# The RWKV rounds of a hybrid decoder layer: a new order of operations on TensorE, VectorE and ScalarE

## What is computed

```python
def step(s, inp):                      # s: state of a head, 64 x 64
    r_t, w_t, k_t, v_t, a_t, b_t = inp
    sa = jnp.einsum('bhij,bhj->bhi', s, a_t)
    s = s * w_t[:, :, None, :] + sa[..., None] * b_t[:, :, None, :] + v_t[..., None] * k_t[:, :, None, :]
    return s, jnp.einsum('bhij,bhj->bhi', s, r_t)
...
y = ((y - mean) * lax.rsqrt(var + R_LN_EPS)).reshape(bsz, t, R_WIDTH) * ln_w + ln_b
bonus = jnp.sum(rh * kh * r_k, axis=-1, keepdims=True) * vh
y = y + bonus.reshape(bsz, t, R_WIDTH)
return (y * g) @ w_out, p[:, -1], s_fin
```

## Time and profile before

| | |
|---|---|
| median of 3 runs | 4114.88 us (4113.28 to 4115.73) |
| the profiled execution | 4111.77 us |
| its span | 4109.3 us |
| TensorE / VectorE / ScalarE busy, share of the span | 93% / 58% / 38% |
| rounds of the RWKV stage | from 2139 us to 2721 us of the span |

### The profile page before, as it was taken

How to read it: one execution, slowest core, us unless ns; L and a number is a source line. 1 busy time by engine, 2 the same in 40 slices (tenths; PEclk the granted TensorE clock), 3 DMA queues, 4 the chain that set the end, 5 groups by cost and what they waited for, 6 DMA issues and landing times. The chain is left out here.

```text
span 4109.3 us, 87073 instructions
## 1 busy us (share of the span) xinstructions
PE 3808.0 (93%) x37206; PEld 3472.0 (84%) x37206; DVE 2370.5 (58%) x4637; ACT 1574.3 (38%) x2857; POOL 195.6 (5%) x203
## 2 busy tenths in 40 slices
PE   8999999999999999889978888879999999999998
PEld 4889999998888889889966666669876899999997
DVE  4445646432588885358966666646643564444446
ACT  3113232232476653334426666544522431111112
POOL 0000000000011111010000000000111100000000
PEclk9999999999999999999989999989999999999999
DMA  5323222243565543655641111042323131111112
GB/s 209 91 87 94 89 89 89 83 112 120 157 155 165 155 136 117 184 150 192 224 145 32 33 36 36 24 162 96 115 89 121 48 103 47 42 44 50 42 32 85
DMA packets 375550, 418.84 MB, mean 102 GB/s; under 512 B 50474, under 2 KB 317276, under 8 KB 374300
## 3 DMA queue, kind: packets, MB, share of 16 engines
q1 hardware_dynamic: 362927, 368.14, 29.3%
q0 software_dynamic: 7632, 27.84, 2.3%
q10 hardware_dynamic: 4608, 17.30, 1.1%
HBM read 289.10 MB, written 121.77 MB: 100 GB/s over the span
## 5 line engine op out<-in xcount | busy, mean ns | idle before, releaser
L248 PE MATMUL bank<-xn_hi,pw_whi 128*128 128x352 f32 (+1 forms) x2184 | 728.8, 334 | 14.9 <-ACT ring L261 7.2
L248 PE MATMUL bank<-xn_hi,pw_wlo 128*128 128x352 f32 (+1 forms) x2184 | 705.8, 323 | 0.0
L248 PE MATMUL bank<-xn_lo,pw_whi 128*128 128x352 f32 (+1 forms) x2184 | 705.0, 323 | 0.0
L248 PEld LDWEIGHTS bank<-xn_hi,pw_whi 128*128 128x128 f32 (+1 forms) x2184 | 411.7, 189 | 38.8 <-issue 24.2
L248 PEld LDWEIGHTS bank<-xn_lo,pw_whi 128*128 128x128 f32 (+1 forms) x2184 | 413.0, 189 | 3.1 <-issue 1.9
L248 PEld LDWEIGHTS bank<-xn_hi,pw_wlo 128*128 128x128 f32 (+1 forms) x2184 | 411.8, 189 | 1.3
L261 ACT ACTIVATE ring<-bank 128x352 f32<-128x352 f32 (+1 forms) x273 | 126.0, 462 | 433.9 <-PE bank L248 433.2
L3214 PE MATMUL bank<-bx_hi,bp_whi 128*128 128x384 f32 (+1 forms) x768 | 269.6, 351 | 18.4 <-DVE bx_lo L3275 15.6
L1804 PE MATMUL bank<-sum_x_hi,pw_whi 128*128 128x352 f32 x768 | 254.1, 331 | 31.1 <-DVE sum_x_lo L1795 13.9
L233 DVE TENSOR_TENSOR pw_wlo<-ring,pw_whi 128x1024 fp32r<-128x1024 f32 (+1 forms) x92 | 117.9, 1282 | 240.1 <-ACT pw_whi L226 239.7
L3851 PE MATMUL bank<-bx_hi,bp_whi 128*128 128x384 f32 (+1 forms) x768 | 251.2, 327 | 4.7 <-issue 4.7
(11 more groups left out here) (719 smaller groups left out, 10690.8 us busy)
## 6 DMA issues: line engine op xcount, KB each, us to landing
ring<-in_w_in_dram SPq DMA_DIRECT2D x90, 512.0 KB, 4.8
proj_scratch<-ring SPq DMA_DIRECT2D x66, 528.0 KB, 3.0
mm_all<-proj_scratch SPq DMA_DIRECT2D x40, 512.0 KB, 6.0
mm_all<-acum_scratch SPq DMA_DIRECT2D x32, 512.0 KB, 6.7
ring<-in_mlp_w_dram SPq DMA_DIRECT2D x16, 1024.0 KB, 5.4
ring<-in_mlp_w_dram SPq DMA_DIRECT2D x32, 512.0 KB, 3.5
gates_scratch<-ring SPq DMA_DIRECT2D x24, 528.0 KB, 6.4
merged_scratch<-sum_gate ACTq DMA_DIRECT2D x24, 528.0 KB, 4.9
```

The lines of the kernel that those rows point to most:

```text
L248: last = self.nc.tensor.matmul(ps[0:n, 0:m], w[:, q, 0:n], self.pair[x][:, q, t0:t0 + m], start=q == 0 and j == 0, stop=q == KD - 1 and j ...
```

## The change

Every part's operations are placed by tables of ticks, 280 to a round, instead of 28 slots, and each engine has a table of its own. A tick below zero (or above 279) puts the operation into the iteration before (or behind). Operations that stood together under one slot are parted: the three masks of the gram step on VectorE (`part` 0 to 2), the two copies of `rows_kb` and of `rows_vd` on ScalarE, the two exponentials of the decay (`ex`, `decays`), the logarithm and the exponential behind it (`k_log`, `k_rs`, with a semaphore in the place of a drain), the square and the copy of `Finish`. The first gram of a round, the first copies and sigmoids of `Prepare` and its first product are issued at the end of the iteration before. The receptance and the key change their order on VectorE and their temporaries. The instructions, their shapes and their number stay; the SyncE and GpSimd programs stay. In the diff one line of three of the tables stands for them; the conversions of the other methods are of the same kind as the two shown.

```diff
-SLOTS = 28
+TICKS = 280
...
-INVERSION = [("gram", "v", 0), ("rows_kb", "a", 3), ("rows_vd", "va", 5), ("square", "va", 7), ("fourth", "va", 10), ("eighth", "v", 13),
-             ("by8", "v", 15), ("turn", "va", 17), ("cross1", "v", 20), ("cross2", "v", 22)]
...
+def at(**ops):
+
+    return {tick % TICKS: (name, -(tick // TICKS)) for name, tick in ops.items()}
...
+SCAN_DVE = at_chunks({(0, 0): 6, (1, 0): 35, (2, 0): 66, (3, 0): 95, (4, 0): 125, (5, 0): 155, (6, 0): 185, (7, 0): 215})
...
+PREPARE_PE = at(lw=-24, la=7, k_sum=75, bon=137)
+PREPARE_ACT = at(key_scale=-54, decay=-31, receptance_scale=-27, value_scale=-24, a=-20, k_sq=17, a_scaled=42, ex=63, decays=104, k_log=118, k_rs=127)
...
-    def scalar(self, act, r, slot):
-        if not 0 <= r < ROUNDS:
+    def scalar(self, act, r, tick):
+        op, ahead = PREPARE_ACT.get(tick, (None, 0))
+        r += ahead
+        if not 0 <= r < ROUNDS or op is None:
             return
...
-        elif slot == 7:
+        elif op == "ex":
             self.nc.scalar.preload_act_table_set("natural_log_exp_and_others")
             act.wait_ge(self.cum, r + 1)
             activation(v.ex[:, :, 1:1 + RC], T[1].rearrange("p (c t) -> p c t", t=RC), ACT.Exp, scale=-KAPPA)
+        elif op == "decays":
             activation(T[4], T[1], ACT.Exp, scale=KAPPA).then_inc(self.decays, 1)
-        elif slot == 8:
+        elif op == "k_log":
             act.wait_ge(self.k_sum, r + 1)
-            activation(T[5], bank[:, :], ACT.Ln, bias=k.eps[:, 1:2])
-            act.drain()
+            activation(T[5], bank[:, :], ACT.Ln, bias=k.eps[:, 1:2]).then_inc(self.k_logged, 1)
+        else:
+            act.wait_ge(self.k_logged, r + 1)
             activation(T[5], T[5], ACT.Exp, scale=-0.5).then_inc(self.k_rs, 1)
...
         @block.scalar
         def _(act):
-            for q in range(-1, ROUNDS + 2):
-                for slot in range(SLOTS):
-                    invert.scalar(act, q, slot)
-                    scan.scalar(act, q - 1, slot, finish.stored)
-                    prepare.scalar(act, q + 1, slot)
-                    finish.scalar(act, q - 2, slot)
+            for q in range(-2, ROUNDS + 3):
+                for tick in range(TICKS):
+                    invert.scalar(act, q, tick)
+                    scan.scalar(act, q - 1, tick, finish.stored)
+                    prepare.scalar(act, q + 1, tick)
+                    finish.scalar(act, q - 2, tick)
```

More of the change, by code:

```diff
@@ L1121, with at_chunks @@
-EACH = {w: sum(w in who for _, who, _ in INVERSION) for w in "va"}
+INVERSION = [("gram", "v"), ("rows_kb", "a"), ("rows_vd", "va"), ("square", "va"), ("fourth", "va"), ("eighth", "v"), ("by8", "v"),
+             ("turn", "va"), ("cross1", "v"), ("cross2", "v")]
+STEP = {name: s for s, (name, _) in enumerate(INVERSION)}
+EACH = {w: sum(w in who for _, who in INVERSION) for w in "va"}
+def at(**ops):
+    return {tick % TICKS: (name, -(tick // TICKS)) for name, tick in ops.items()}
+def at_chunks(ops):
+    return {tick % TICKS: (step, -(tick // TICKS)) for step, tick in ops.items()}
@@ new lines, in at_both @@
+def at_both(*ops):
+    return {tick % TICKS: ((name, p, part), -(tick // TICKS)) for name, part, ticks in ops for p, tick in enumerate(ticks)}
+INVERT_PE = at_both(("gram", 0, (-21, 6)), ("rows_kb", 0, (11, 29)), ("rows_vd", 0, (34, 61)), ("square", 0, (90, 96)), ("fourth", 0, (118, 130)),
+                    ("eighth", 0, (148, 154)), ("by8", 0, (162, 170)), ("turn", 0, (180, 191)), ("cross1", 0, (204, 220)),
+                    ("cross2", 0, (225, 253)))
+INVERT_DVE = at_both(("gram", 0, (-8, 12)), ("gram", 1, (5, 16)), ("gram", 2, (10, 20)), ("rows_vd", 0, (73, 89)), ("square", 0, (114, 123)),
+                     ("fourth", 0, (133, 145)), ("eighth", 0, (153, 156)), ("eighth", 1, (154, 157)), ("by8", 0, (165, 182)),
+                     ("turn", 0, (199, 204)), ("cross1", 0, (206, 220)), ("cross1", 1, (216, 234)), ("cross2", 0, (236, 260)))
@@ L1124, in evacuated @@
+PREPARE_DVE = at(zero=-84, key=-12, receptance=27, value=31, cum=65, k_a=72, bon=124, k_n=128, b_a=143, bonus=147, AR_r=167, PC=168, AR_a=183, B=186,
+                 K=200)
+FINISH_PE = at(mean=155, var=195, gate=226)
+FINISH_ACT = at(square=169, centre=186, log=219, rstd=220)
+FINISH_DVE = at(scale=229, bias=233, gate=235)
 def evacuated(r, s, who):
-    return r * EACH[who] + sum(who in w for _, w, _ in INVERSION[:s + 1])
+    return r * EACH[who] + sum(who in w for _, w in INVERSION[:s + 1])
@@ L1171, in tensor @@
         at, T = slice(n * RW, (n + 1) * RW), v.T
-        if slot == 0:
+        if op == "lw":
             if r >= 1:
@@ L1392, in vector @@
-        last.then_inc(self.vs[p], 1)
-    def scalar(self, act, r, slot):
-        if not 0 <= r < ROUNDS or slot not in STEPS:
+        if part == 0:
+            if "a" in INVERSION[s][1]:
+                dve.wait_ge(self.as_[p], evacuated(r, s, "a"))
+            else:
+                dve.wait_ge(self.pes[p], r * len(INVERSION) + s + 1)
+        if step == "gram" and part == 0:
+            tt(v.ABR[:, w, c, :], wide(b0), mask(v.m_a), ALU.mult)
+        elif step == "gram" and part == 1:
+            tt(x.O[:, :, :], wide(b0)[:, :, 0:RC], mask(v.m_cross), ALU.mult)
+        elif step == "gram":
+            tt(v.KX[:, w, c, :], wide(b1), mask(v.m_k), ALU.mult).then_inc(self.vs[p], 1)
+        elif step == "rows_vd":
+            plus_one(x.X, 0).then_inc(self.vs[p], 1)
+        elif step in ("square", "fourth"):
+            plus_one(x.P, 1).then_inc(self.vs[p], 1)
+        elif step in ("eighth", "cross1") and part == 0:
+            plus_one(x.P, 0)
+        elif step in ("eighth", "cross1"):
+            copy(halves(x.X), self.product(p, 1)).then_inc(self.vs[p], 1)
+        elif step == "by8":
+            copy(halves(x.X), self.product(p, 0)).then_inc(self.vs[p], 1)
+        elif step == "turn":
+            plus_one(x.P, 0).then_inc(self.vs[p], 1)
+        else:
+            copy(v.N[:, w, c, :].rearrange("p (q e) n -> p e q n", e=2),
+                 self.product(p, 0).rearrange("p e (q n) -> p e q n", n=RC)).then_inc(self.vs[p], 1)
@@ L1396, in scalar @@
+    def scalar(self, act, r, tick):
+        if tick not in INVERT_ACT:
             return
-        s, p = STEPS[slot]
-        if "a" not in INVERSION[s][1]:
+        op, ahead = INVERT_ACT[tick]
+        r += ahead
+        if not 0 <= r < ROUNDS:
             return
+        step, p, part = op
         v = self.v
-        step, x, c = INVERSION[s][0], v.inv[p], slice(p * BATCH, (p + 1) * BATCH)
+        s, x, c = STEP[step], v.inv[p], slice(p * BATCH, (p + 1) * BATCH)
         b0, b1 = self.banks(p)
@@ L1440, in carried, with tensor @@
         return n - n // 16
-    def tensor(self, pe, r, slot, vs, as_):
+    def tensor(self, pe, r, tick, vs, as_):
+        if tick not in SCAN_PE:
+            return
+        op, ahead = SCAN_PE[tick]
+        r += ahead
         if not 0 <= r < ROUNDS:
```

263 lines of the change are left out of this document (138 added, 125 removed).

## The result

| | us |
|---|---|
| changed kernel, median of 4 runs | 4092.55 (4090.26 to 4096.15) |
| kernel before, median of 4 runs beside it | 4114.08 (4112.27 to 4115.73) |
| ratio | 0.9949, 95% interval 0.9931 to 0.9966 |
| the profiled execution, and its span | 4096.15, 4094.0 |

Faster by 21.5 us, where 84 were forecast. The time lies outside the range, on its upper side, by 16.5 us.

The account below looks back on a forecast made before the run. The order of the chained hops, not a full engine, bounds the kernel. Rounds 1 to 13 save 74.9 us, round 0 4.8, the last but one 4.5, in all 84.2: 4031 us predicted, range 4003 to 4076.

Parts of the forecast that it names:

- TensorE needs about 20.5 us a round: Steady rounds: TensorE's products priced by array time sum to about 20.5 us, so no engine is full in 34.16 us.
- the pass by hand: Steady round worked through in the new order, each engine taking its list: 26.35 us, against 33.5 in round 6 before.
- If U waits where I gave it only the bare hop: Scan, U copy: a sign that the prediction is wrong, U waiting beyond the priced hop of 0.43 us.
- chunks 0, 1: Start of a round's scan: 3.4 and 2.45 us, together 5.85 where they took 6.79.
- chunk 2: Scan chunk where the table load delayed the state's copy: 2.65 us where it was 5.77.
- the allowance: Steady round: +2 us on the hand sum for small waits left out, bounds 0.5 and +5, giving 28.4 us.
- The table load: ScalarE, chunk 2: load moved behind a state's copy, mostly under hops; load 1.28 us without drain, U about 0.7 us late.
- Chunks 3 to 6: Middle of the scan: chunks 3 and 4 take 6.3 us (were 9.06), chunks 5 and 6 take 5.55 (were 6.71).
- The turn: Chunk 7 into the next round: 6.0 us where it was 5.18, the one place that grows.
- The clock: Steady rounds: half-speed stretches go, granted clock at or near 1.00 where it was 0.93.
- Rounds 0 and 14: First and last but one rounds: 27.6 us from 32.4 (saving 4.8), and 25 from 29.5 (saving 4.5).
- Rival (a): Steady rounds: queues lock at more places than seen, rounds of 31.3 us, 4074 us in all; chance 0.18.

Follow-up runs that it names:

- all steps joined: Changed kernel, also called few instructions: each inversion step's products joined into one wide product per array corner, inversion left out of the result; 4013.72 us, ratio 0.9757.
- one batch joined: Changed kernel with only batch 0's inversion-step products joined into wide ones, that batch's inversion left out of the result; 4019.23 us, ratio 0.9776.
- `fourth` joined: Changed kernel with only the inversion step `fourth` joined into wide products in both batches, fourth power left out of the result; 4052.41 us, ratio 0.9854.
- one batch padded: Batch 0's inversion products joined in the changed kernel, the replaced products put back ahead with one moving column each; 4134.51 us, ratio 1.0053.
- the burst: Changed kernel plus 640 64-column and 320 128-column products without waits ahead of the rounds, on four corners; 3.47 to 3.75 us a block from the second stand.

## Why the prediction was wrong

**The step that failed** is "TensorE needs about 20.5 us a round (an estimate from these rows). No engine is full in 34.16 us." The passes were priced at the array's pace. Their instructions also have to be brought, in blocks of 256 that take 3.47 to 3.75 us, which makes 26.8 to 28.9 us a round. Over against the pass by hand of 26.35 us this leaves no slack, and a stretch of dense inversion steps uses its instructions up faster than the next come: there stand 4.2 of the 5.3 us. In the prediction's own terms, the price of TensorE in chunks 3 to 6 had no term for this. Five kernels of the new order on one scale (supply, an estimate: weight loads of the window rows, as many products and 43 semaphore instructions, at 3.47 to 3.75 us for 256):

| kernel (new order) | weight loads a round | supply, us | stands, us | round, us |
|---|---|---|---|---|
| all steps joined | 470 | 13.3 to 14.4 | 0.3 | 27.26 |
| one batch joined | 719 | 20.1 to 21.7 | 0.3 | 27.78 |
| `fourth` joined | 887 | 24.6 to 26.6 | 2.2 | 30.08 |
| the changed kernel | 966 | 26.8 to 28.9 | 5.3 | 32.99 |
| one batch padded | 1047 | 29.0 to 31.3 | 3.3 | 35.58 |

Up to some 21 us of supply the round hardly depends on it; beyond, it rises, 5.2 us for some 7 of supply from one batch joined to the changed kernel. That is the threshold that the half joining showed; it lies between the second row and the third. The 2.6 us more of the padded kernel are in part its own passes. A stand of TensorE comes out as a wait of the hops: U comes 1.3 to 1.5 us behind R in chunks 4 to 6, where a bare hop is 0.43 and with few instructions it is 0.4 to 0.7. "If U waits where I gave it only the bare hop" was one of the prediction's own signs of being wrong, and it is the one that came.

**The pass by hand was right for what it priced**, part by part, and the kernel with few instructions shows it:

| us | forecast | changed kernel | few instructions |
|---|---|---|---|
| chunks 0, 1 | 5.85 | 6.39 | 6.10 |
| chunk 2 | 2.65 | 3.11 | 2.77 |
| chunks 3, 4 | 6.3 | 8.18 | 6.17 |
| chunks 5, 6 | 5.55 | 8.19 | 5.64 |
| turn | 6.0 | 7.13 | 6.58 |
| round | 26.35, 28.4 with the allowance | 32.99 | 27.26 |

- *The table load*: right, in place and price. By itself, in the old order, it is worth 34 us.
- *Chunks 3 to 6*: short by 4.5 us. Here lie the dense steps of the inversion, and with few instructions both terms are met within 0.15.
- *The turn*: mis-sized by 0.6 even with few instructions. ScalarE's timeline of round 6's turn shows the wait that the pass left out:

```profile
2410.91 0.59 ACT L1588 ACTIVATE ring<-bank 128x512 f32<-128x512 f32 x1
2413.20 1.28 ACT L1252 ACT_TABLE_LOAD   x1 [1.70 <-PE bank L1217]
2414.50 0.69 ACT L1252 ACTIVATE r_work<-bank,vec 128x512 f32<-128x512 f32 x1
...
2417.34 0.23 ACT L1575 ACTIVATE r_U<-bank 128x64 f32<-128x64 f32 x1
```

  The load stands idle 1.70 us for the decay's product, although it needs nothing of it; to put it first brought some 3 us, since the second sigmoid, ahead of the U of chunk 0, then waits for its own product instead (0.3 and 1.4 us in rounds 6 and 9 of that run), and R to U of chunk 0 hardly changed, 2.10 us from start to start against 2.20.
- *The clock*: right, 0.93 to 1.00. It comes with the table load alone too.
- *Rounds 0 and 14*: 30.6 and 28.5 us, forecast 27.6 and 25. With 13 x (32.99 - 28.4) = 59.7 this makes 66 us above the forecast; the median is 61.5 above it, and the profiled execution, from which these places are read, is 3.6 above the median.
- *Rival (a)*, 31.3 us a round at a chance of 0.18, was the nearest in size, but its reason, locked queues, was not the cause: with few instructions the same order has 27.26.

The Trainium skill, "Runtime: NRT & Kernel Launch", section "Instruction fetch mechanics", says that instructions come in 16 KiB blocks of 256 and that crossing a block is mostly hidden. The traces agree with the block (128 weight loads and their products, one transfer of 16 KB). They do not agree with the hiding: 1.5 to 1.8 us a block in the burst, 62.6 us at the blocks' edges in the steady rounds. The Trainium skill, "ScalarE: Activation LUTs", section "What ACT_TABLE_LOAD costs", has a drain behind the load; in the changed kernel, too, none is seen (0.01 us).

What stays open: why a burst's blocks take 3.47 us in some places and 3.75 in others, and how much of the 4.6 us between the forecast round and the measured one is stands and how much other waits; the stands in chunks 3 to 6 are 4.2 us, and the joined kernels change both. Whether a correct kernel in the new order can do with fewer and wider products was not tried.

## What to carry to other kernels

Price TensorE twice, once by columns and once by instructions: where it has many small products on four corners at once, 128 weight loads with their products cost about 3.5 us here, and an order that takes away its waits runs into that. The sign of it in a profile is "issue" in front of weight loads that have no wait, at one and the same place of every 256 instructions of the queue. In the kernel before it was there, but small (7.7 us). And try the largest single part of a reordering alone: here it was worth 34 us, and the whole 21.5.

## What the runs showed of the hardware

- TensorE's instructions arrive by 16 KB transfers of 256; in a burst on four corners a block of 128 weight loads and 128 products takes 3.47 to 3.75 us, of which the array needs 1.95; on two corners (3.73 us) no stand is seen.
- All 53 stands of over 0.5 us of the changed kernel lie at one place of every 256 instructions; such a stand ends 2.2 to 2.9 us after the start of a transfer that itself takes 0.9 to 1.5 us.
- In the changed kernel, with 5.3 us of stands a round, 1.7 us more array work a round cost nothing (4092.34 against 4092.55).
- A pass of one column holds TensorE as long as one of 64: 58 ns from start to start in both.
